# Block products in the gated layers: chunks 3 to 8 as three pairs, and the low half of the down weights by an accumulating load

## The reference

```python
def swiglu(h, wg, wu, wd):
    return (jax.nn.silu(h @ wg) * (h @ wu)) @ wd
# per layer l of 2 (D_MODEL 1024, D_FF 2816, 256 tokens)
h = rmsnorm(x, g[0])
x = x + 0.5 * rmsnorm(swiglu(h, ffn_wg[l, 0], ffn_wu[l, 0], ffn_wd[l, 0]), g[1])
...   # attention
h = rmsnorm(x, g[4])
x = x + 0.5 * rmsnorm(swiglu(h, ffn_wg[l, 1], ffn_wu[l, 1], ffn_wd[l, 1]), g[5])
```

## Time and profile before

| | |
|---|---|
| runs | 1428.69, 1423.15, 1429.99 us |
| profiled execution, its own time | 1423.64 us |
| its span, first to last instruction | 1421.9 us |
| TensorE matmul | 1373.9 us busy, 97% of the span |
| VectorE | 1097.4 us, 77% |
| ScalarE | 821.3 us, 58% |
| GpSimd | 80.4 us, 6% |
| granted TensorE clock, mean | 0.994 |

### The profile page before, as it was taken

The page is one execution under the profiler, slowest core; times in us unless marked ns, Lnnn a source line. Parts: engine busy times, 40 slices in busy tenths (PEclk is TensorE's granted clock), DMA queues, the critical chain, the costliest instruction groups (busy, mean ns, idle before and its releaser), DMA issues. The chain is left out here.

```text
span 1421.9 us, 19388 instructions
## 1 busy us (share of the span) xinstructions
PE 1373.9 (97%) x6943; PEld 1139.1 (80%) x6943; DVE 1097.4 (77%) x1565; ACT 821.3 (58%) x1301; POOL 80.4 (6%) x133
## 2 busy tenths in 40 slices
PE   4999999999999999999999999999999999999998
PEld 4878877999987778887778778887878877787786
DVE  5677787799776998579986998569986546679883
ACT  4456755755446565466576556465664567566561
POOL 3011100000000000021300000000000100000000
PEclk9999999999999999999999999999999999999999
DMA  9887556486644566644355476535656363564570
GB/s 353 290 297 254 192 174 192 144 281 237 225 160 154 186 208 210 208 133 149 114 164 184 147 237 225 189 129 184 235 183 231 125 210 118 192 207 149 178 236 30
DMA packets 160702, 274.37 MB, mean 193 GB/s; under 512 B 5953, under 2 KB 87617, under 8 KB 160609
## 3 DMA queue, kind: packets, MB, share of 16 engines
q1 hardware_dynamic: 153904, 250.86, 52.6%
q0 software_dynamic: 5552, 20.20, 4.4%
q10 hardware_dynamic: 1153, 2.07, 0.4%
HBM read 272.05 MB, written 1.06 MB: 192 GB/s over the span
## 5 line engine op out<-in xcount | busy, mean ns | idle before, releaser
L2331 DVE TENSOR_TENSOR w_lo<-raw,w_hi 128x1024 fp32r<-128x1024 f32 (+2 forms) x310 | 368.3, 1232 | 71.5 <-ACT w_hi L2069 70.4
L2069 ACT ACTIVATE w_hi<-raw 128x1024 fp32r<-128x1024 f32 (+2 forms) x310 | 308.5, 1047 | 94.8 <-PE psum L2804 32.9
L2802 PE MATMUL psum<-w_hi,hT_hi 128*128 128x512 f32 x712 | 287.5, 404 | 6.3 <-DVE hT_lo L2496 3.7
L2804 PE MATMUL psum<-w_hi,hT_lo 128*128 128x512 f32 x712 | 278.3, 391 | 0.0
L2803 PE MATMUL psum<-w_lo,hT_hi 128*128 128x512 f32 x712 | 278.2, 391 | 0.0
L2802 PEld LDWEIGHTS psum<-w_hi,hT_hi 128*128 128x128 f32 x712 | 134.8, 189 | 38.5 <-issue 10.0
L2804 PEld LDWEIGHTS psum<-w_hi,hT_lo 128*128 128x128 f32 x712 | 134.6, 189 | 29.0
L2803 PEld LDWEIGHTS psum<-w_lo,hT_hi 128*128 128x128 f32 x712 | 135.1, 190 | 25.8 <-issue 0.7
L2802 PE MATMUL psum<-w_hi,hc_hi 128*128 128x512 f32 x272 | 107.5, 395 | 1.8 <-DVE hc_lo L2421 1.2
L2804 PE MATMUL psum<-w_hi,hc_lo 128*128 128x512 f32 x272 | 106.1, 390 | 0.0
L2803 PE MATMUL psum<-w_lo,hc_hi 128*128 128x512 f32 x272 | 106.0, 390 | 0.0
(11 more groups left out here) (301 smaller groups left out, 2801.4 us busy)
## 6 DMA issues: line engine op xcount, KB each, us to landing
raw<-in_ffn_wd_dram SPq DMA_DIRECT2D x44, 1024.0 KB, 5.0
raw<-in_ffn_wg_dram SPq DMA_DIRECT2D x56, 512.0 KB, 4.1
raw<-in_ffn_wu_dram SPq DMA_DIRECT2D x56, 512.0 KB, 5.4
raw<-in_w_up_dram SPq DMA_DIRECT2D x44, 512.0 KB, 4.9
raw<-in_w_in_dram SPq DMA_DIRECT2D x19, 1024.0 KB, 7.4
raw<-in_ffn_wg_dram SPq DMA_DIRECT2D x16, 1024.0 KB, 5.1
raw<-in_ffn_wu_dram SPq DMA_DIRECT2D x16, 1024.0 KB, 5.1
ada_raw<-in_w_ada_dram POOLq DMA_DIRECT2D x24, 512.0 KB, 5.3
```

What stands on the lines that cost most here:

```text
L2069: nc.scalar.activation(hi_of(s)[:, cs], source_of(s)[:, cs], ACT.Copy).then_inc(ready, 1)
L2331: nc.vector.tensor_tensor(lo_of(u)[:, cs], source_of(u)[:, cs], hi_of(u)[:, cs].bitcast(F32), ALU.subtract)\
L2802: nc.tensor.matmul(o, a_hi, b_hi, start=start, stop=False)
L2804: return nc.tensor.matmul(o, a_lo, b_hi, start=False, stop=stop)
```

## The change

1. `GROUPS = (3, 5, 7)`: chunks 3, 4 and 5, 6 and 7, 8 are groups, in a row; singles are 0, 1, 2, 9, 10. A group that follows a group takes the two turns of the one before after its u1 and its u5, and does both down units of the pair before (after u6 and after u2). Two single chunks in each gated layer become one group; the total of units grows by 12.
2. `LOADED`: the down units of chunks 0 to 8 of each gated layer have no low half by VectorE. ScalarE writes minus the high half (128 x 2048, one instruction) into the low slot, and GpSimd issues a load of the raw weights from HBM that adds into it. TensorE waits for its landing. The raw buffer of such a unit is free once its high half is made.
3. `token_sums` and `token_high` stand right after the turn of chunk 1, `token_low` before the down unit in chunk 2, and the splits ahead in chunk 2 go one unit less far (`less`).

```diff
-GROUPS = (4, 7)
+GROUPS = (3, 5, 7)
+LOADED = (0, 1, 2, 3, 4, 5, 6, 7, 8)
...
         def down_unit(self, c):
             self.downs[c] = pl.unit(2, D, [(0, D, rows(self.w_down, 2 * c, 2, 0, D))])
+            if c in LOADED and not self.conv:
+                pl.low_loaded.append(self.downs[c])
...
             self.hidden_turn(1)
+            pl.add("token_sums")
+            pl.add("token_high")
             c = 2
...
+                less = 1 if c + 1 in GROUPS else 0
                 self.up(c, 0)
                 if after_group:
                     self.group_turn(c - 2, 0)
-                self.up(c, 1)
-                if after_group:
                     self.group_turn(c - 2, 1)
+                self.up(c, 1, less)
                 self.out(c)
                 if c == 2:
-                    pl.add("token_sums")
-                    pl.add("token_high")
+                    pl.add("token_low")
                 if after_group:
                     self.down(c - 2)
-                self.down(c - 1)
+                self.down(c - 1, less)
                 self.hidden_turn(c)
-                if c == 2:
-                    pl.add("token_low")
...
+            close = c - 2 in GROUPS
             product_of(u1, p1, True, tile=(0, 0), mixed=None)
+            if close:
+                self.group_turn(c - 2, 0, banks[3])
             product_of(u5, p5, True, tile=None, mixed=3)
+            if close:
+                self.group_turn(c - 2, 1, banks[3])
             pl.add("gkeep", use=p1, slot=0)
             product_of(u7, p7, True, tile=None, mixed=2)
             pl.add("gkeep", use=p5, slot=1)
+            p6 = pl.use(banks[3], u6)
             product_of(u6, p6, True, tile=None, mixed=0)
             pl.add("gsum", kept=(p1, p5), uses=(p6, p7), n=n)
-            self.down(c - 1)
+            self.down(c - 2 if close else c - 1)
...
             pl.add("ggate", t=0, use=p2, stat=self.st, n=n)
+            if close:
+                self.down(c - 1)
...
                         sp.wait_ge(hi_ready, until + 1)
-                        sp.wait_ge(lo_ready, until + 1)
+                        if until not in plan.low_loaded:
+                            sp.wait_ge(lo_ready, low_until(until))
...
+                elif kind == "split_hi" and a["unit"] in plan.low_loaded:
+                    i = plan.low_loaded.index(a["unit"])
+                    pool.wait_ge(minus_ready, i + 1)
+                    nk, w, parts = units[a["unit"]]
+                    pool.dma_start(lo_of(a["unit"]).rearrange("p (k n) -> p k n", k=nk), parts[0][2], accum_op=ALU.add)\
+                        .then_inc(low_landed[i % 8], 16)
...
+                if s in plan.low_loaded:
+                    act.wait_ge(hi_ready, s + 1)
+                    nc.scalar.activation(lo_of(s), hi_of(s).bitcast(F32), ACT.Copy, scale=-1.0).then_inc(minus_ready, 1)
...
                 if s >= len(units):
                     return
+                if s in plan.low_loaded:
+                    return
                 form(s + 1)
...
                     pe.wait_ge((hi_half_ready, hi_ready)[half], u + 1)
-                    pe.wait_ge((lo_half_ready, lo_ready)[half], u + 1)
+                    if u in plan.low_loaded:
+                        i = plan.low_loaded.index(u)
+                        pe.wait_ge(low_landed[i % 8], 16 * (i // 8 + 1))
+                    else:
+                        pe.wait_ge((lo_half_ready, lo_ready)[half], low_until(u))
```

More of the change, by code:

```diff
@@ L146, in __init__ @@
         self.formed, self.raw_from, self.release = {}, {}, {}
+        self.low_loaded = []
         self.n_group, self.last_sum = 0, None
@@ L852, in down_step, with down, down_part, up @@
             pl.add("down", c=c, unit=self.downs[c], uses=self.y, gs=self.gs, pick=pick, done=done)
-        def down(self, c):
+        def down(self, c, less=0):
             self.down_unit(c)
-            self.down_part(c)
-        def down_part(self, c):
-            pl.split_ahead(self.downs[c])
+            self.down_part(c, less)
+        def down_part(self, c, less=0):
+            pl.split_ahead(self.downs[c], less)
             self.down_step(c, [(k, t, half) for k in range(2) for t in range(TT) for half in range(2)], True)
-        def up(self, c, i):
+        def up(self, c, i, less=0):
             if c not in self.units:
@@ L867, in up @@
             p = self.parts[c][i]
-            pl.split_ahead(p["unit"])
+            pl.split_ahead(p["unit"], less)
             product_step("up", p)
@@ L937, in group @@
             banks = (4, 5, 6, 7) if c % 2 == 0 else (6, 7, 4, 5)
-            p1, p5, p7, p6 = (pl.use(b, u) for b, u in zip(banks, (u1, u5, u7, u6)))
+            p1, p5, p7 = (pl.use(b, u) for b, u in zip(banks, (u1, u5, u7)))
+            close = c - 2 in GROUPS
             product_of(u1, p1, True, tile=(0, 0), mixed=None)
+            if close:
+                self.group_turn(c - 2, 0, banks[3])
             product_of(u5, p5, True, tile=None, mixed=3)
+            if close:
+                self.group_turn(c - 2, 1, banks[3])
             pl.add("gkeep", use=p1, slot=0)
@@ L961, in group, with group_turn @@
             self.group_no = n
-        def group_turn(self, c, t):
-            made = pl.turned_use((7 if c % 2 == 0 else 5) - t)
+        def group_turn(self, c, t, bank=None):
+            made = pl.turned_use((7 if c % 2 == 0 else 5) - t if bank is None else bank)
             pl.add("gturn", c=c, t=t, n=self.group_no, down_before=self.downs[c - 1], **made)
@@ L1745, in program @@
         stored = sem("stored")
+        minus_ready, low_landed = sem("minus_ready"), [sem(f"low_landed{i}") for i in range(8)]
         sum_ready = sem("sum_ready")
@@ L1845, in source_of, with low_until @@
             return raw_of(plan.raw_from.get(u, u))
+        def low_until(u):
+            return u + 1 - sum(1 for v in plan.low_loaded if v <= u)
         def half_of(u, half):
@@ L2316, in form @@
                         dve.wait_ge(hi_ready, made["last"] + 1)
-                        dve.wait_ge(lo_ready, made["last"] + 1)
+                        dve.wait_ge(lo_ready, low_until(made["last"]))
                 if made["no"]:
```

## The result

The changed kernel takes 1626.45 us (median of six runs, 1619.22 to 1628.46) against 1426.53 us of the kernel before (six runs beside it): a ratio of 1.139, 95% interval 1.1371 to 1.1409. The forecast was 1540 us with a range to 1585. The sign holds, and so do the places of the waits: TensorE stands in the row of groups and ahead of the loaded down units.

A forecast was written before the change was run, and what follows sets the result against it. TensorE multiplies in 97% of the span, with VectorE at its limit in each group; 34.0 us of waits, less matmuls saved, made each layer 29.2 us later, 117 in four, on 1423.64: 1540 us, range 1465 to 1585.

The forecast's parts named there:

- the place of VectorE's idle time ahead of form u5: Third group: VectorE idle 5.2 us ahead of form u5, for a load issued after the low half of u4.
- the second `ggate` of the first group: VectorE's gate of the second token tile, forecast done at 522.6 us; turn 1 then waits 1.3 us for it.
- L: Time from the minus copy's end to landing of the accumulating load: 6 us, with 5 and 10.5 as ends.
- the walk: Order followed through the first gated layer: 34.0 us of waits, 29.2 us later per layer; 1510 to 1585, chance 0.60.
- turn 1 of the third group: TensorE's wait in the third group for VectorE's ggate, done at 566.7: 6.0 us.
- turn 0 of the second: TensorE's wait after u1 of the second group for VectorE's ggate at 518.1: 5.0 us.
- swallowed where VectorE sets the time: L = 10.5 adds 4.5 us at down 0 but is swallowed later: 34 per layer, 1559 us.
- the second bound: Upper bound with L = 10.5 and a slower clock on top: 1585 us.
- rival 4: Adding load doesn't keep pace, L of 15 and more, or it slows SyncE's loads: above 1585 us, chance 0.06.
- rival 3: Clock falls in TensorE's waits: 38 us, 1578 if none is swallowed, most expected to be; within the walk's 0.60.
- rival 1: VectorE keeps up, second ggate of the first group done by 507 us; only landings and saving left: 1419 us, chance 0.09.
- Rival 2: VectorE's busy time alone binds, loads and minus copies hide: 1467 to 1510 us, chance 0.18.

The follow-up runs named there:

- turn_first: Changed kernel with the split of the next down unit behind turn 0 instead of ahead of it in a group that closes another: 1629.89 us.
- g3_both: Three groups in a row without accumulating loads, raw buffers reloaded once the sum is formed, next down unit's split behind turn 0: 1503.75 us, 1.0542 against the kernel before.

## Why the prediction was wrong

**Held.** The matmul count, the price of the minus copy, the place of VectorE's idle time ahead of form u5 (8.0 us, where 5.2 were forecast), and the second `ggate` of the first group (522.6 forecast, 526.95 measured, of which the longer wait at down 0 is 2.8). With loads that land about when I assumed (5.5 us from issue, 7.3 on average from the minus copy, where L was 6) the kernel takes 1543.8 us; the walk gave 1540. That agreement is in good part luck, since errors hide within it: over the four layers that run waits 27.7 us for landings, where the walk had 77, and 73.2 for the turns, where it had 58, and its slow matmuls of 25.6 us weren't in the sum at all. By its own single waits the walk had turn 1 of the third group at 6.0 (9.8 is the longest wait there in that run), and turn 0 of the second at 5.0 (1.62 in the changed kernel).

**The term that was mis-sized: L, the accumulating load.** It stood at 6 us, nearest to loads that don't add; it measures 9.2 from issue, 11.0 on average from the minus copy. No row showed an adding load. The rows to weigh more were the two of 8.4 and 10.5 us in the earlier trace rows, which I set aside as crowded. This size alone doesn't explain the miss: the walk had a bound for L = 10.5.

**The step that failed with it: "swallowed where VectorE sets the time".** I had bounded L = 10.5 at 1559 us, 34 us per layer against the 29.2 of L = 6, and the clock on top at 1585. The runs with delayed plain loads show 51 us for 1.8 us of lateness and 64 for 5.4, and the changed kernel lies 41 us above the second bound. The walk treated the landing as a wait of TensorE alone and every other load as fixed at 5.0 us. In fact the loads that VectorE's forms need became late with it: VectorE's idle time for them is 74.4 us after, 56.8 and 64.4 with plain loads made late, 41.8 with plain loads, 34.6 without loads. VectorE, which was to swallow the wait, thus stood longer itself. Two ways lead there, and the runs don't divide them: a late down unit holds its slots of halves longer by the kernel's order, and a load that is moved or slow shares its time with SyncE's. Slower loads of SyncE beside the adding ones were rival 4, at 0.06; they are in the rows (7.3 and 10.0 us), and its place above 1585 was right.

**Overlooked: one bank for both turns.** The low half of turn 0 stands between the turns, and ScalarE's order ahead of it. It is the largest named wait (58.1 us). An earlier turn 0 gained nothing beside the late loads (turn_first) and 9.3 us without them (g3_both); a bank of its own for each turn was not tried.

**The clock (rival 3).** Slow matmuls grew by 38.6 us in the gated layers, where its price was 38. The sum had put it at nothing, expecting most to be swallowed. Counted along TensorE's own time line it isn't nothing: of the 83 us above the forecast, 38.6 are slow matmuls, 22 are landings (99.3 us where the walk had 77) and 9 are turns (66.7 where it had 58). With plain loads slow matmuls stand at 25.6 us, with late ones at 38.9 and 40.8. That TensorE ran slower so long is in the rows; how much of it reaches the end isn't shown, since the one run on it was undecided.

**Rivals 1 and 2.** `ggate` of the first group wasn't done by 507 us, the mark of rival 1. Rival 2's limit, VectorE's busy time alone, wasn't contradicted as a floor: it began at 1467, and the best forms of three groups took 1482.9 (spaced) and 1503.8 us (in a row).

**Small slips.** Rival 1 reckons four waits of 4.2 us at down 0, its L = 5 value; at L = 6 it is 5.2, and the sum 1423 instead of 1419. The earlier trace rows shows no slower slice at the start; the slow stretch there is in the earlier trace rows. And the 3.50 us of idle didn't bring that clock about by themselves: from 25 to 28 us, of which TensorE was idle all but the first 0.32, it is already 0.57 on average, and ahead of this stood matmuls of one column. The lower level behind waits is shown by the changed kernel instead.

## What to carry to other kernels

A low half that comes by an adding load is late by the load's whole length, and it slows the loads beside it: price it from a run of one such load in the crowd where it will stand, not from plain loads. When a profile is full of waits that name each other, don't take the largest named one for the term: look first where waits without a name end (27 us here ended with a landing), and take one away at a time, since here most of what was taken from the largest stood again further on. And before a delay is called swallowed, follow what the late engine releases (slots, buffers, banks) back to the engine that is to swallow it.

## What the runs showed of the hardware

- A 1024 KB load that adds into the on-chip buffer, issued by GpSimd, landed 9.2 us after issue (median; 8.5 at the least, 12.1 among other loads in the order of before); the same without adding 5.5 (8.5 there). The issue itself took GpSimd 1.19 us against 0.71 (medians).
- With 64 of each 1024 columns the adding load landed in 3.1 us.
- Beside adding loads, SyncE's loads of 1024 KB rose from 5.0 to 7.3 us, 5.1 to 6.3, and 6.3 to 10.0 (medians, the run with plain loads against the changed kernel); the longest took 16.0 us. Plain loads from GpSimd made late by five operations brought the last of these from 6.3 to 8.3 us as well.
- Behind waits of 5 to 10 us the first matmuls started 0.43 us apart instead of 0.23, the lower clock level (behind one of 5.20 us for three steps, behind one of 7.96 us for more than seven), and the mean granted clock of the span fell from 0.994 to 0.944.
